# A two-layer encoder kernel: value projection last among the query products, first GEMM step of each stage by halves of the tokens

## What is computed

```
for layer in range(DEPTH):
    g = norm_gains[layer]
    h = h + 0.5 * rms_norm(swiglu(rms_norm(h, g[0]), ffn_w_in[layer, 0], ffn_w_out[layer, 0]), g[1])
    hn = rms_norm(h, g[2])
    m = attention_mixer(hn, ...) if layer % 2 == 0 else recurrent_mixer(hn, ...)
    h = h + rms_norm(m, g[3])
    h = h + 0.5 * rms_norm(swiglu(rms_norm(h, g[4]), ffn_w_in[layer, 1], ffn_w_out[layer, 1]), g[5])
return h[:, N_META:]
```

## Time and profile before

| | us |
|---|---|
| median of 3 runs | 1080.57 (1079.9 to 1081.22) |
| the profiled execution | 1080.62 |
| its span | 1078.7 |
| PE busy in it | 1057.7 |
| DVE, ACT, POOL busy in it | 687.5, 547.0, 88.7 |

### The profile page before, as it was taken

The page is one execution under the profiler, slowest core; times in us unless marked ns, Lnnn a source line. Parts: engine busy times, 40 slices in busy tenths (PEclk is TensorE's granted clock), DMA queues, the critical chain, the costliest instruction groups (busy, mean ns, idle before and its releaser), DMA issues.

```text
span 1078.7 us, 20692 instructions
## 1 busy us (share of the span) xinstructions
PE 1057.7 (98%) x8454; PEld 1027.8 (95%) x8454; DVE 687.5 (64%) x998; ACT 547.0 (51%) x790; POOL 88.7 (8%) x88
## 2 busy tenths in 40 slices
PE   8999999999999999999999999999999999999997
PEld 8999999999779999999999999999999999999986
DVE  6766656477774866664467666644698668667652
ACT  5544454454675544434446444444568855454541
POOL 3000000026100200000010000000224210000000
PEclk9999999999999999999999999999999999999999
DMA  9554446635104255435653554366328425655541
GB/s 304 187 194 157 136 148 199 220 118 163 44 2 132 91 186 179 156 126 189 195 194 118 176 194 156 108 210 209 118 80 271 160 79 172 204 172 190 194 143 40
DMA packets 160912, 170.17 MB, mean 158 GB/s; under 512 B 3265, under 2 KB 154105, under 8 KB 160841
## 3 DMA queue, kind: packets, MB, share of 16 engines
q1 hardware_dynamic: 160456, 168.70, 48.1%
q0 software_dynamic: 96, 0.28, 0.1%
q10 hardware_dynamic: 288, 0.18, 0.1%
HBM read 167.82 MB, written 1.05 MB: 157 GB/s over the span
## 4 chain that ended last, share of the span: by engine, by line
PE 88%; DVE 6%; ACT 3%; DMA 1%; POOL 1%; issue 1%; SPq 0%; DVEq 0%; POOLq 0%; ACTq 0%
PE bank L449 23%; PE bank L451 23%; PE bank L450 23%; PE bank L838 5%; PE bank L659 2%; PE bank L658 2%; PE bank L660 2%; DVE h L1378 1%; DVE xl L1341 1%; PE flipped L755 1%; PE weighed L767 1%; DMA raw<-in_rec_w_in 1%; DVE mg L1374 1%; DVE wl L1335 1%; PE bank L501 1%; POOL hacc L1824 1%
## 5 line engine op out<-in xcount | busy, mean ns | idle before, releaser
L1335 DVE TENSOR_TENSOR wl<-raw,wh 128x2048 fp32r<-128x2048 f32 (+2 forms) x164 | 340.5, 2098 | 161.0 <-ACT wh L937 160.7
L449 PE MATMUL bank<-xh,wl 128*128 128x272 f32 (+1 forms) x1504 | 435.6, 290 | 2.0 <-DVE xl L1604 1.1
L451 PE MATMUL bank<-xh,wh 128*128 128x272 f32 (+1 forms) x1504 | 432.4, 288 | 0.0
L450 PE MATMUL bank<-xl,wh 128*128 128x272 f32 (+1 forms) x1504 | 431.1, 287 | 0.0
L937 ACT ACTIVATE wh<-raw 128x2048 fp32r<-128x2048 f32 (+2 forms) x164 | 282.2, 1744 | 104.5 <-PE bank L451 82.6
L449 PEld LDWEIGHTS bank<-xh,wl 128*128 128x128 f32 x1504 | 283.8, 189 | 3.6 <-issue 2.3
L451 PEld LDWEIGHTS bank<-xh,wh 128*128 128x128 f32 x1504 | 283.8, 189 | 0.0
L450 PEld LDWEIGHTS bank<-xl,wh 128*128 128x128 f32 x1504 | 283.7, 189 | 0.0
L449 PE MATMUL bank<-ah,wl 128*128 128x272 f32 x528 | 152.1, 288 | 0.0
L450 PE MATMUL bank<-al,wh 128*128 128x272 f32 x528 | 151.9, 288 | 0.0
L451 PE MATMUL bank<-ah,wh 128*128 128x272 f32 x528 | 151.7, 287 | 0.0
(11 more groups left out here) (197 smaller groups left out, 1214.1 us busy)
## 6 DMA issues: line engine op xcount, KB each, us to landing
raw<-in_ffn_w_in SPq DMA_DIRECT2D x88, 1024.0 KB, 5.3
raw<-in_ffn_w_out SPq DMA_DIRECT2D x24, 768.0 KB, 5.0
raw<-in_ffn_w_out SPq DMA_DIRECT2D x24, 640.0 KB, 4.4
raw<-in_ffn_w_out SPq DMA_DIRECT2D x10, 1024.0 KB, 5.2
raw<-in_rec_w_in SPq DMA_DIRECT2D x8, 1024.0 KB, 5.4
raw<-in_attn_w_qkv SPq DMA_DIRECT2D x6, 1024.0 KB, 4.9
raw<-in_attn_w_o SPq DMA_DIRECT2D x4, 1024.0 KB, 5.2
raw<-in_rec_gate_w SPq DMA_DIRECT2D x16, 256.0 KB, 5.8
```

Source lines behind the costliest of these rows:

```text
L449: pe.matmul(dst, b, mh, start=first, stop=False)
L450: pe.matmul(dst, a, ml, start=False, stop=False)
L451: return pe.matmul(dst, a, mh, start=False, stop=last)
L1335: dve.tensor_tensor(wl[:, slot(u), 0:kn * 256], w, wh[:, slot(u), 0:kn * 256].bitcast(F32), ALU.subtract).then_inc(w_ready, units)
```

## The change

Five things are changed.

1. In the stages n = 1 to 5, `residual`, `make_x`, `sum_squares` and `chunk` run by halves of the tokens: first all eight chunks for columns 0 to 135, then all eight for 136 to 271 (in the last stage 16 to 143 and 144 to 271).
2. Attention's first step has four tiles (two of keys, two of queries), and the value products stand behind the last query tile, in its own weight unit, which is now loaded last. The later tiles, their head means and the weight splits have new places, and some banks are exchanged.
3. `rc_of_h`, the reciprocal, now stands ahead of the weight split `low(u0 + 3)` and the clearing of the sum, which move from the end of the stage before into `ffn`.
4. In FFN 0 `mean_of_h` and `spread_r` are put later, the second two tiles are made by `product`, and ACT splits weight unit 3 before it squares chunks 2 to 7.
5. DVE's low part of the third output unit (`U_WO + 2`) and a clearing of the sum move from the query tiles into softmax step 10; ACT's high part of it moves into softmax step 0.

```diff
-                pe.wait_ge(xh_ready, KC * norm + k + 1)
+                t, new = slice(*halves(norm)[half]), k == 0 and half == 0
+                pe.wait_ge(xh_ready, x_index(norm, half, k) + 1)
...
-                    pe.matmul(dst, b, xh[:, k, t0:L], start=k == 0, stop=False)
-                    pe.matmul(dst, a, xh[:, k, t0:L], start=False, stop=False)
...
+                    for half in range(2):
+                        for k in range(KC):
+                            last = chunk([(dst, u, 2 * k + m) for dst, u, m in tiles[0] + tiles[1]], k, X_OF_FFN[n], half)
...
-                            if f == f0 + 2 and part == 0 and k == 3:
+                            if n == 0 and f == f0 + 2 and part == 0 and k == 7:
+                                mean_of_h(0)
+                            if f == f0 + 2 and (part, k) == ((0, 3) if n else (1, 6)):
                                 spread_r(X_OF_FFN[n])
...
+                pe.wait_ge(w_ready, U_VAL + 1)
+                for c in range(3):
+                    for k in range(KC):
+                        last = values(c, k)
+                        if (c, k) == (0, 4):
+                            mean_and_rotation(QKT - 1)
+                        if (c, k) == (0, 7):
+                            pe.wait_ge(q_gained, QKT)
+                            scores(1)
+                    last.then_inc(v_done, 1)
...
+                for half in range(2):
+                    for c in range(KC):
+                        scale(c, half)
+                        add(c, half)
+                        if c >= 1:
+                            low_x(n, c - 1, half)
+                    low_x(n, KC - 1, half)
...
+                rc_of_h(X_OF_FFN[n])
+                if n:
+                    low(u0 + 3, 0)
+                    clear_sum()
                 r_of_h(X_OF_FFN[n])
...
+                    if s == 0:
+                        value(2)
+                        dve.wait_ge(v_ready, 3)
+                        dve.memset(vt[0:OVERLAP, 2, :], 0.0).then_inc(v_ready, 1)
+                    if s == 10:
+                        low(U_WO + 2, 0)
+                        clear_sum()
...
             h_square(0, 1)
             high(2, 0)
+            high(3, 0)
             for c in range(2, KC):
                 h_square(0, c)
-            high(3, 0)
```

More of the change, by code:

```diff
@@ L71 @@
 NPROJ = 6
+PROJ_T0 = [META if n >= 4 else 0 for n in range(NPROJ)]
 WARM = 18
@@ L125, in last_factor, with halves, x_index @@
     return 3 * (KT_N + 2 * j + (1 if q in (0, 3, 4) else 0)) + 3
+def halves(n):
+    t0 = PROJ_T0[n - 1]
+    mid = (t0 + L) // 2
+    return (t0, mid), (mid, L)
+def x_index(n, half, c):
+    return 8 + 16 * (n - 1) + 8 * half + c if n else c
 def shape_constants():
@@ L457, in keep_warm, with chunk @@
                     pe.matmul(dst[:, 0:P], ident, ident, start=True, stop=True)
-            def chunk(tiles, k, norm, t0, values=None, done=None):
-                pe.wait_ge(xh_ready, KC * norm + k + 1)
+            def chunk(tiles, k, norm, half, done=None):
+                t, new = slice(*halves(norm)[half]), k == 0 and half == 0
+                pe.wait_ge(xh_ready, x_index(norm, half, k) + 1)
                 for dst, u, tile in tiles:
                     a, b = (v[:, slot(u), tile * P:(tile + 1) * P] for v in (wh, wl))
-                    pe.matmul(dst, b, xh[:, k, t0:L], start=k == 0, stop=False)
-                    pe.matmul(dst, a, xh[:, k, t0:L], start=False, stop=False)
[L467 to L475, removed]
+                    pe.matmul(dst[:, t], b, xh[:, k, t], start=new, stop=False, skip_group_check=True)
+                    pe.matmul(dst[:, t], a, xh[:, k, t], start=False, stop=False, skip_group_check=True)
+                pe.wait_ge(x_ready, x_index(norm, half, k) + 1)
+                last = [pe.matmul(dst[:, t], wh[:, slot(u), tile * P:(tile + 1) * P], xl[:, k, t], start=False, stop=k == KC - 1,
+                                  skip_group_check=True) for dst, u, tile in tiles]
+                if done is not None and k == KC - 1 and half:
                     for product_done in last:
@@ L678, in attention @@
                 pe.wait_ge(w_ready, U_QKV + 2)
[L679 to L685, removed]
+                for half in range(2):
+                    for k in range(KC):
+                        chunk([(qk_bank(t)[:, 0:L], U_QKV + t // 2, 2 * k + t % 2) for t in range(4)], k, 1, half, qk_done)
                 mean_of_h(1)
@@ L847, in recurrent @@
                 pe.wait_ge(w_ready, U_REC + 2)
-                for k in range(KC):
-                    last = chunk([(REC_BANKS[REC_ORDER[j]][m][:, 0:L], U_REC + j, 2 * k + m) for j in range(2) for m in range(2)],
-                                 k, 4, 0)
+                for half in range(2):
+                    for k in range(KC):
+                        last = chunk([(REC_BANKS[REC_ORDER[j]][m][:, 0:L], U_REC + j, 2 * k + m) for j in range(2) for m in range(2)],
+                                     k, 4, half)
                 for product_done in last:
@@ L1142, in attention @@
                 root(0)
+                squared(2)
                 root(1)
[L1144 to L1151, removed]
+                squared(3)
+                high(U_QKV + 5, 0, KC, (qk_done, 4))
+                root(2)
+                squared(4)
+                root(3)
+                squared(5)
+                high(U_WO, 0, KC, (qk_done, 6))
+                root(4)
+                squared(6)
+                root(5)
+                root(6)
+                squared(7)
+                high(U_WO + 1, 0, KC, (qk_done, 8))
+                root(7)
+                squared(8)
+                root(8)
+                squared(9)
+                root(9)
                 load_table(ACT.Exp)
@@ L1559, in attention @@
                 dve.wait_ge(rsq_ready, 1)
-                for t in range(KT_N):
+                dve.wait_ge(norm_q_ready, 2)
+                for t in range(QKT - 1):
                     head_root_in(t)
```

218 lines of the change are left out of this document (114 added, 104 removed).

## The result

The changed kernel takes 1120.29 us (median, 1119.39 to 1120.49) against 1080.62 us for the kernel before in the same series: a ratio of 1.0369, 95% interval 1.0355 to 1.0383. It is slower by 39.7 us; the prediction was 1119.5. The profiled execution has a span of 1118.7 us.

What follows compares the result with a forecast made beforehand. The prediction took TensorE (PE), busy 98% of the span, as the bound. Its terms, +46.0 - 2.0 - 2.9 - 0.5 - 1.5 = +39.1 us on 1080.6, gave 1119.7, called 1119.5, with a range of 1108 to 1130.

Steps and rivals of the forecast that it cites:

- Part 1: Five first steps by halves: 960 narrow instructions at 0.112 us, 107.5 us for 61.5 before, cost +46.0 us.
- Part 2: Starts of the five first steps: half chunks let PE start about 0.4 us earlier each, -2.0 us.
- Part 3: Reciprocal ahead of the weight split: PE's waits for reciprocal (2.1 us) and last-stage split (0.8) go, -2.9 us.
- Part 4: The opening, with the mean 24 products later: -0.5 us, ends -3.3 (no wait and full clock) and +1.
- Part 5: Attention, value products last: net 3.2 - 1.0 (query-tile wait) - 1.2 (softmax split), rounded to -1.5 us, ends -5 and +2.
- A: Rival for the halved products: loads hide fully and streamed columns set the price, kernel ends at 1075.9 us; chance 0.05.
- rival D: First steps: DVE or ScalarE becomes the bound; 48 DVE operations are 14 us against 21.5 of PE; chance 0.02.
- C: Rival: clock falls inside the longer first steps, 1127 us with one stretch each, 1204 throughout; chance 0.06 for over 1130.

Runs made afterwards that it cites:

- e1_whole: The changed kernel with only the halves undone, so first steps run over whole rows of tokens again: 1077.71 us.
- e2_load64: The changed kernel with the halved products loading only 64 of 128 weight columns, the other output rows left out: 1099.26 us.
- e3_move64: The changed kernel with the halved products moving only 64 token columns instead of 136, with full weight loads: 1210.98 us.
- e4_rc_behind: The changed kernel with the reciprocal put back behind the weight split and the clearing of the sum, on DVE only: 1120.47 us.
- e5_before_rc: The kernel before with only the reciprocal put ahead of the weight split and the clearing, in whole-token steps: 1076.71 us, ratio 0.9974 to before.
- e6_best: e1_whole with the old opening put back and the weight split and clearing of softmax step 10 moved behind the last softmax step: 1076.45 us.
- e8_opening: e6_best with the mean late, the fourth unit's high part after six squares and the spread nine products after the mean: 1073.17 us.

## Why the prediction was right, point by point

The parts below are taken from the two profiled executions by stage. They add up to the 40.1 us between the two spans.

**Part 1, the narrow steps: right in mechanism and size.** 960 instructions at 0.112 us were forecast and measured, 107.3 us against the 107.5 of the sum; the steps before come to 61.9 instead of 61.5, since attention's 96 take 12.5 us in a step of their own (e1_whole). The term is +45.4 for +46.0. That the load sets it was argued from plain fp32 rows; e2_load64 and e3_move64 show it for the fp32r products themselves. The 81 ns that the Trainium skill gives, cited there, are not met by this kernel.

**Part 2, the earlier start: right.** From the start of the last filler product to the first of the step were 0.63 us before and are 0.23 after; five times 0.4 is the forecast 2.0. PE now comes straight from the filler products.

**Part 3, the reciprocal: undersized, and the cause not separated.** The waits for the reciprocal and for the split went, but e4_rc_behind shows that in this kernel the longer step removed them and the move did nothing. The prediction named both causes and did not separate them. The size was off as well: what FFN 1, FFN 2 and FFN 3 fall short of the 9.0, 9.0 and 9.5 us of their longer steps, the earlier starts taken into account, is 0.9, 0.8 and 2.1, so -3.8 us for -2.9. The move alone, without the halves, gave 0.9 + 0.9 + 1.1 = 2.9 (e5_before_rc). That this is the forecast figure is luck: the forecast was 2.1 for three waits for the reciprocal and 0.8 for the split, and the wait for the split is still there in e5_before_rc; the rest is the 0.27 us per stage beyond the waits.

**Part 4, the opening: +0.8 instead of -0.5.** Both stalls forecast are there (1.4 us for the sum, 1.1 for the scaling). The half clock at about 30 us is in the traces of before, after, e2_load64 and e3_move64, but not in the others: e4_rc_behind and e1_whole have the opening of after, e5_before_rc that of before with the same pause, and none of them has it. So it is not a property of the order, and counting on its loss or return was wrong. Between traces without it the two openings differ by at most 0.3 us: from the first product after the wait for weights to attention's first step are 202.0 us in e5_before_rc and e6_best, 202.0 in e1_whole and 201.3 in e4_rc_behind, in which that step starts 0.4 us earlier by the halves.

**Part 5, values last: the forecast -1.5 is about -0.7 in the trace.** Attention grew by 7.9 us where the step and its start account for 8.6. The two pieces are read one by one: the new order gives 1.7 us (e6_best against e5_before_rc) instead of the net 2.2 forecast for it, although the wait early in the query tiles, forecast at about 1 us, is only 0.17; and the split in the softmax takes 1.7 instead of 1.2. That would leave about 0; the other 0.5 us is in e5_before_rc too, whose attention has the order of before and is 0.5 us shorter. It lies between 279.6 and 295.7 us of before, where both traces have a half-clock stretch, but at 281.9 in one and 279.8 in the other; that its place makes the difference is likely and not shown. Each piece misses by 0.5 us, within the ends given.

**What half clock costs.** The prediction took each stretch of about 3.4 us at half clock in before as some 1.7 us lost. In the two later series before ran 27 times: the 14 executions with a mean granted clock of 0.999 took 1079.0 to 1079.9 us, the 13 at 0.996 or 0.997 took 1079.9 to 1081.6. The means of the two groups are 1.5 and 1.0 us apart in the two series. The profiled execution of before, with both stretches, has 0.996. So two stretches cost together less than the forecast took for one, as far as the mean clock tells which executions had them.

**The rivals.** A (streaming sets the price) is out, and its time of 1075.9 would have been wrong even with light loads: e2_load64 takes 1099, since DVE then decides. That was rival D, priced at 14 us a step from 48 operations of 0.3 us; DVE is busy 14.9 us and the step takes 16.4. C (the clock falls in the steps) did not come at 136 columns, but my argument against it, that PE does not pause, is refuted by e3_move64: the clock fell there without any pause. The chance for it was set too low for the reason given. Its price of 0.2 us at half clock was near: 0.213 is measured.

The sum of +39.1 meets the 40.1 of the traces, and 1119.5 the measured 1120.3, partly because errors cancel: 0.6 too much in Part 1 and 0.9 too little gain in Part 3 stand against 1.3 and 0.8 too much gain in Parts 4 and 5, and 0.3 in the recurrent stage for which there was no part (e1_whole and e8_opening have it too, e5_before_rc and e6_best don't).

## What to carry to other kernels

Splitting a matmul's moving columns doubles its weight loads; read from the trace what a load costs in a row (here 0.112 us for 128 columns) and do not go below the number of columns that takes as long to stream (here about 240, an estimate from 272 columns at 0.126 us and 0.43 ns a column). What starts earlier by such a split is worth one latency per stage (0.4 us here), what it costs is paid for every instruction (9 us a stage). When several edits come in one change, undo the largest alone: here 42.6 us of loss hid 2 us of gain, and with it gone and two weight splits and the opening placed by the waits the kernel came to 1073.2. When two edits could remove the same wait, try each without the other: the reciprocal's move was worth 3 us in one kernel and nothing in the other.

## What was not expected of the hardware

- With 64 moving columns and full weight loads, the granted clock fell to 0.50 within a step in which PE had work without a pause; with 136 (and with 128 in the last stage) it stayed at 1.00. So a PE that the profile shows as fully busy was not at full clock each time.
- At half clock the distance of load-bound instructions went from 0.112 to 0.213 us, so weight loads slow down with the clock too.
- Before had a half-clock stretch of 3.4 us behind a wait of 1.67 us in the opening, e5_before_rc none behind 1.69 us in the same opening: one trace doesn't show that a pause makes the clock fall each time.
- Halving the columns of a DVE operation does not halve it: the scale of 272 columns takes 0.44 us, that of 136 takes 0.28; the add of 136 takes 0.30, and up to 0.60 beside a GpSimd sum. The slow ones exist with 272 columns too: the add 0.44 or up to 0.73, the low part 0.50 or up to 1.02 us, the scale never more than 0.44.
